# The order of ScalarE's work within a slot, and later slots for the norms, in an fp32 encoder trunk whose weights are split as they stream in

## The reference, cut to what matters

```python
def reference(...):                       # 512 prompt frames and 32 sample frames, D_MODEL = 1024, fp32
    for layer in range(2):
        g = norm_g[layer]
        xp, xs = rms_norm(hp, g[0]), rms_norm(hs, g[0])
        # layer 0: gated MLP and sliding-window attention with one output projection
        # layer 1: trailing mean pooling (windows 2, 4, 8, 16), then c_w, 4 groups of 256x256
        ...
        hp = hp + rms_norm(mp, g[1])
        hs = hs + rms_norm(ms, g[1])
        hp = hp + rms_norm(swiglu(rms_norm(hp, g[2]), ffn_w_in[layer], ffn_w_out[layer]), g[3])
        hs = hs + rms_norm(swiglu(rms_norm(hs, g[2]), ffn_w_in[layer], ffn_w_out[layer]), g[3])

def swiglu(h, w_in, w_out):               # w_in 1024 x 5632, w_out 2816 x 1024
    gu = h @ w_in
    return (jax.nn.silu(gu[..., :D_FF]) * gu[..., D_FF:]) @ w_out
```

## Time and profile before

| | |
|---|---|
| median of 3 runs | 1091.4 us (1090.87 to 1092.74) |
| the profiled execution | 1087.63 us, its span 1085.3 us |
| granted TensorE clock, mean | 0.994 |
| TensorE busy | 1045.7 us (96%) |
| VectorE busy | 623.3 us (57%) |
| ScalarE busy | 511.4 us (47%) |
| GpSimd busy | 50.8 us (5%) |
| HBM | 149 GB/s over the span |

### The profile page before, as it was taken

One profiled execution on the slowest core, in us unless ns is written; L12 is line 12 of the kernel. 1 busy time (PEld: TensorE's weight loads), 2 busy tenths in 40 slices (PEclk: granted clock), 3 DMA queues, 4 the chain that ended last, 5 costly groups with the idle time before them and its releaser, 6 DMA issues.

```text
span 1085.3 us, 19346 instructions
## 1 busy us (share of the span) xinstructions
PE 1045.7 (96%) x8087; PEld 1019.9 (94%) x8087; DVE 623.3 (57%) x920; ACT 511.4 (47%) x837; POOL 50.8 (5%) x52
## 2 busy tenths in 40 slices
PE   6999999899999999999989889999999999999997
PEld 4798889899999999999989889999999999999996
DVE  4377855777555545544456666667754545454543
ACT  5531355556444444445456445564544444444542
POOL 0070220000000000000000000200000000000000
PEclk9999999999999999999999999999999999999998
DMA  7413113456665555546654465454565555466552
GB/s 244 98 44 103 40 40 97 138 155 195 195 190 170 165 166 165 159 140 188 179 154 129 132 186 165 129 166 133 164 198 161 170 158 164 145 182 179 152 169 82
DMA packets 307636, 162.47 MB, mean 150 GB/s; under 512 B 14553, under 2 KB 304321, under 8 KB 307550
## 3 DMA queue, kind: packets, MB, share of 16 engines
q1 hardware_dynamic: 305678, 159.11, 50.3%
q10 hardware_dynamic: 1648, 1.78, 0.5%
q0 software_dynamic: 224, 0.35, 0.1%
HBM read 158.63 MB, written 2.58 MB: 149 GB/s over the span
## 4 chain that ended last, share of the span: by engine, by line
PE 78%; DVE 10%; issue 6%; ACT 3%; DMA 1%; POOL 1%; SPq 0%; ACTq 0%; DVEq 0%; POOLq 0%
PE ps L529 25%; PE ps L530 24%; PE ps L531 24%; DVE wlo L1435 3%; ACT whi L1049 2%; DVE tmp L1701 1%; DVE h L1705 1%; PE ps L569 1%; DMA x_tok<-in_x_sample_dram 1%; POOL rs L1946 1%; DVE acc L1687 1%; PE ps L786 1%; PE ps L946 0%; DVE tmp L1715 0%; PE ps L918 0%
## 5 line engine op out<-in xcount | busy, mean ns | idle before, releaser
L1435 DVE TENSOR_TENSOR wlo<-raw,whi 128x1024 fp32r<-128x1024 f32 (+2 forms) x332 | 369.0, 1112 | 309.1 <-ACT whi L1049 308.4
L529 PE MATMUL ps<-xhi,whi 128*128 128x288 f32 (+1 forms) x1600 | 466.5, 292 | 8.7 <-DVE wlo L1435 6.5
L530 PE MATMUL ps<-xlo,whi 128*128 128x288 f32 (+1 forms) x1600 | 462.9, 289 | 0.0
L531 PE MATMUL ps<-xhi,wlo 128*128 128x288 f32 (+1 forms) x1600 | 460.5, 288 | 0.0
L1049 ACT ACTIVATE whi<-raw 128x1024 fp32r<-128x1024 f32 (+2 forms) x332 | 315.1, 953 | 222.2 <-PE ps L531 191.2
L529 PEld LDWEIGHTS ps<-xhi,whi 128*128 128x128 f32 x1600 | 302.4, 189 | 12.2 <-DVE wlo L1435 7.4
L531 PEld LDWEIGHTS ps<-xhi,wlo 128*128 128x128 f32 x1600 | 302.8, 189 | 0.0
L530 PEld LDWEIGHTS ps<-xlo,whi 128*128 128x128 f32 x1600 | 302.6, 189 | 0.0
L529 PE MATMUL ps<-mhi_b,whi 128*128 128x288 f32 x352 | 105.7, 300 | 5.5 <-DVE wlo L1435 5.5
L531 PE MATMUL ps<-mhi_b,wlo 128*128 128x288 f32 x352 | 104.3, 296 | 0.0
L530 PE MATMUL ps<-mlo_b,whi 128*128 128x288 f32 x352 | 102.7, 292 | 0.0
(11 more groups left out here) (216 smaller groups left out, 944.8 us busy)
## 6 DMA issues: line engine op xcount, KB each, us to landing
raw<-in_ffn_w_in_dram SPq DMA_DIRECT2D x176, 512.0 KB, 3.9
raw<-in_ffn_w_out_dram SPq DMA_DIRECT2D x64, 384.0 KB, 3.5
raw<-in_ffn_w_out_dram SPq DMA_DIRECT2D x64, 320.0 KB, 3.1
raw<-in_ab_w_in_dram SPq DMA_DIRECT2D x10, 512.0 KB, 4.0
raw<-in_ab_w_out_dram SPq DMA_DIRECT2D x10, 256.0 KB, 2.8
raw<-in_ab_w_out_dram SPq DMA_DIRECT2D x20, 128.0 KB, 3.1
x_tok<-in_x_prompt_dram SPq DMA_DIRECT2D x4, 512.0 KB, 5.2
raw<-in_ab_w_in_dram SPq DMA_DIRECT2D x8, 256.0 KB, 3.5
```

The source lines that it names most:

```text
L529: pe.matmul(out, wh, xh, start=first, stop=False)
L530: pe.matmul(out, wh, xl, start=False, stop=False)
L531: return pe.matmul(out, wl, xh, start=False, stop=last)
L1435: dve.tensor_tensor(wlo[:, s, 0:n], raw[:, m % NRAW, 0:n], whi[:, s, 0:n].bitcast(F32), ALU.subtract)\
```

## The change

ScalarE's `square_pair` and `x_high` yield their slot plus 0.5 (`LATER`), and all passes call `run(slot + LATER)` behind `hi_part(m + 4)` (in odd slots of `ffn_in`, behind the high part of the product too). Squares and x high parts thus follow the slot's weight high part. VectorE's last `x_low` moves one slot on. In `STAGE`, the three stages of half 1 get two slots between `sum` and `spread` and between `pre` and `again` (in place of one), and what follows moves back by one to five slots; the `c` units of layer 1 come after units 22 and 24 in place of 19 and 21. In `after_mixer_ab` two of ScalarE's squares go behind a high part, and on VectorE the low parts of units + 9, + 10 and + 11 go behind the fold of the squares.

```diff
--- before.py
+++ after.py
@@ -81,17 +81,17 @@
 CARRY = 16
 
 
-C_AFTER = ((15, 16), (19, 21))
+C_AFTER = ((15, 16), (22, 24))
 STAGE = {
-    (0, 1): {"sum": 1, "spread": 2, "scale": (3, 5, 7, 9), "fold": 10, "pre": 12, "again": 13, "x": (14, 16, 18, 20)},
+    (0, 1): {"sum": 1, "spread": 3, "scale": (3, 5, 7, 9), "fold": 11, "pre": 13, "again": 15, "x": (15, 17, 19, 21)},
     (1, 0): {"sum": 0, "spread": 1, "scale": (1, 2, 3, 4), "fold": 6, "pre": 8, "rows": (7, 7, 8, 8),
              "keep": (9, 9, 10, 10), "bands": (11, 11, 12, 12, 13, 13, 14, 14)},
     (2, 0): {"sum": 20, "spread": 21, "scale": (21, 22, 23, 24), "fold": 26, "pre": 28, "again": 29,
              "x": (29, 30, 31, 32)},
-    (1, 1): {"sum": 1, "spread": 2, "scale": (2, 3, 5, 6), "fold": 8, "pre": 10, "rows": (8, 9, 9, 12, 12, 13),
-             "keep": (11, 11, 12, 12, 13, 13), "bands": (14, 14, 15, 15, 16, 16, 17, 17, 18)},
-    (2, 1): {"sum": 25, "spread": 26, "scale": (26, 27, 29, 30), "fold": 32, "pre": 34, "again": 35,
-             "x": (35, 36, 38, 39)},
+    (1, 1): {"sum": 2, "spread": 4, "scale": (4, 5, 7, 8), "fold": 10, "pre": 12, "rows": (10, 11, 11, 15, 15, 16),
+             "keep": (14, 14, 15, 15, 16, 16), "bands": (17, 17, 18, 18, 19, 19, 20, 20, 21)},
+    (2, 1): {"sum": 28, "spread": 30, "scale": (30, 31, 33, 34), "fold": 36, "pre": 38, "again": 40,
+             "x": (40, 41, 42, 43)},
     (3, 0): {"sum": 1, "spread": 2, "scale": (2, 4, 6, 8), "rows": (10, 10, 11, 11)},
 }
 
@@ -190,7 +190,7 @@
     return run
 
 
-LAST = 1 << 20
+LAST, LATER = 1 << 20, 0.5
 
 
 def shape_constants():
@@ -1243,11 +1243,11 @@
                 hi_part(U_OUT + 8)
                 square_pair(0, 0, 0)
                 evacuate_out(9)
+                hi_part(U_OUT + 9)
                 square_pair(0, 0, 1)
-                hi_part(U_OUT + 9)
-                square_pair(0, 0, 2)
                 evacuate_out(10)
                 hi_part(U_OUT + 10)
+                square_pair(0, 0, 2)
                 square_pair(0, 0, 3)
                 evacuate_out(11)
                 hi_part(U_OUT + 11)
@@ -1278,6 +1278,7 @@
                         pool_products(m, 1)
                         run(slot)
                         hi_part(m + 4)
+                        run(slot + LATER)
                         continue
                     f, j = divmod(UNITS[m][3], 2)
                     i = inner(layer, b, f)
@@ -1365,7 +1369,7 @@
                 if s == 3:
                     return
                 for p, slot in enumerate(at["scale"]):
-                    yield slot
+                    yield slot + LATER
                     square_pair(s, b, p)
                 if not power:
                     yield at["pre"]
@@ -1738,22 +1742,22 @@
                 add_z(0, 1, 2)
                 residual_pair(0, 0, 1)
                 lo_part(U_OUT + 8)
+                residual_pair(0, 0, 2)
                 add_z(0, 1, 3)
-                residual_pair(0, 0, 2)
-                lo_part(U_OUT + 9)
                 residual_pair(0, 0, 3)
-                add_z(0, 1, 4)
-                lo_part(U_OUT + 10)
                 add_square(0, 0, 3)
                 fold_squares(0, 0)
+                add_z(0, 1, 4)
+                lo_part(U_OUT + 9)
+                invert(0, 0, 1)
                 add_z(0, 1, 5)
-                lo_part(U_OUT + 11)
-                invert(0, 0, 1)
+                lo_part(U_OUT + 10)
                 dve.wait_ge(r_kept[0], KEPT[0, 1])
                 x_scale(0, 0, 0)
+                lo_part(U_OUT + 11)
+                x_low(0, 0, 0)
                 x_scale(0, 0, 1)
                 add_z(0, 1, 6)
-                x_low(0, 0, 0)
                 x_scale(0, 0, 2)
                 x_low(0, 0, 1)
                 lo_part(U_OUT + 12)
@@ -1867,6 +1871,7 @@
                     x_scale(s // 2, b, p)
                     if p:
                         x_low(s // 2, b, p - 1)
+                yield at["x"][-1] + 1
                 x_low(s // 2, b, 3)
 
             def pooling(b):
```

## The result

| | before | after |
|---|---|---|
| median of the runs | 1091.13 us (1089.12 to 1092.74, 4 runs) | 1063.47 us (1062.22 to 1065.39, 4 runs) |
| the profiled execution, its span | 1087.63, 1085.3 us | 1063.66, 1061.4 us |
| granted clock, mean of that execution | 0.994 | 0.996 |
| TensorE busy | 1045.7 us | 1037.8 us |

The ratio is 0.9749, interval 0.9727 to 0.9771: 27.7 us saved by the medians, 24.0 us between the two profiled executions. I had forecast 1071.6 us, a gain of 19.8, and a range that began at 1068. The sign and the mechanism held; the size was too small by 8 us of 28.

A forecast was written before the change was run, and what follows sets the result against it. TensorE, busy 1045.7 of 1085.3 us, was the bound, leaving only waits and lower clock to gain. Terms 3.3 + 6.2 + 1.5 + 2.1 + 7.5 - 0.3 - 0.5 = 19.8 us off 1091.4 gave 1071.6 us, range 1068 to 1078.

The forecast's parts named there:

- the ring: Norm slots passed between VectorE and ScalarE make weight low parts late; reordering in ffn_out(0, 1) removes 3.3 + 6.2 us.
- second drop: Lower clock at 696.92 us behind short matmuls: expected to stay, with 1.3 us as the gain if it falls away.
- the bands: Band low parts held up behind VectorE's product beside GpSimd's multiplication: third ring bank 0.3 us late, once.
- the cost of a wait: Each TensorE wait was taken to cost 0.17 us more than its row says.
- (a): VectorE becomes the bound in ffn_out(0, 1), low parts stay late: gives back 2.8 to 6 us, about 1076 us; chance 0.27.
- (b): ScalarE's order is of no account, only the GpSimd gaps count: 5.6 us gained, 1085.8 us; chance 0.05.
- (c): Squares last in the slot hold up silu or evacuation in ffn_in: 24 us lost, 1095 us; chance 0.04.
- thinnest cover: Second unit's low part at ffn_in(1, 0) ready about 1.2 us before TensorE arrives; failing, part of 2.8 us stays.
- `after_mixer_ab`: Reordering around the fold: no gain expected, a loss of 0.5 us; bounds a gain of 0.5 and a loss of 1.5.
- the step of the clock: Lower-clock time around ffn_in(1, 0): 1.5 us taken as gained, a further 1.3 us drop at 696.92 left in.
- first drop: Lower clock at the start of ffn_in(1, 0), behind the 2.8 us wait: 1.5 us taken as gone, bounds 0 and 1.5.
- the gaps: Two slots for GpSimd's power in (0, 1), (1, 1), (2, 1): 2.1 us with the fold's second wait, then 7.5 us.

The follow-up runs named there:

- order alone: Kernel before, with ScalarE's squares and x high parts behind the slot's weight high part, last x low part one slot later: 1064.95 us, ratio 0.9778.
- the squares alone: Kernel before, with only ScalarE's squares behind the slot's weight high part, x high parts still ahead of it: 1069.72 us, ratio 0.9823.
- old slots: Changed kernel with the stage slots and c units put back as before: 1066.01 us, ratio 0.9763 to the kernel before.
- old `after_mixer_ab`: Changed kernel with the order of after_mixer_ab put back as before: 1063.68 us, ratio 0.9767 to the kernel before.
- the gaps alone: Kernel before, with only the slots of the three stages of half 1 and the c units moved: 1087.11 us, ratio 0.9977.

## Why the prediction was right or wrong, point by point

**Right: the ring.** No low part is late in any of the three passes. `ffn_out(0, 1)`, up to the first matmul of the next pass, gained 10.45 us where I had 3.3 + 6.2 = 9.5; `ffn_in(1, 0)` 11.91 where I had 1.5 + 7.5 - 0.3 = 8.7; `ffn_in(0, 0)` 1.66 where I had 2.1 - 0.5 = 1.6. The surplus of 3.2 us in `ffn_in(1, 0)` is made up of terms below: the second drop of the clock, the bands, the cost of a wait and the pace of the matmuls. The prediction's figures for the scale slots there add up to some 14.7 us of VectorE's work, not 14, against TensorE's 14.1; it held all the same. The run with ScalarE's order alone keeps nearly all of the gain; rivals (a), (b) and (c) are out: VectorE does run without a gap, as (a) had it, but the three units ahead cover it; no silu or evacuation is waited for. The thinnest cover, 1.2 us at the second unit of `ffn_in(1, 0)`, was 1.1: low part ready at 618.65, pass begun at 619.74.

**Right: `after_mixer_ab`.** Sum 0.56 us earlier (0.5 placed), third unit 0.42 later (0.5 placed), two x waits of about 1.1 us between starts in place of one; I had 1.0 and 2.1 for them.

**Wrong: the step of the clock.** This is the term that put the time outside the range. I took 1.5 us for the first drop, left the second (1.3 us) in because the short matmuls ahead of it stay, and carried the sum over to the median as if the 3.8 us between profile and median had nothing to do with the change. The second drop went: in the profiled runs the two drops cost 3.1 us, counted by the starts of the same matmuls, not 1.5. In the four traces with the whole of ScalarE's order (after, order alone, old slots, old `after_mixer_ab`) the clock doesn't fall ahead of the tail. But it didn't fall behind the short matmuls in the unchanged kernel's second trace either, and it did in the one with the squares alone, so that the second drop is gone may in part be chance.

The rest is the way from the profile to the median. The profiled run of before lay 3.5 us below its median, after's at its own. The unchanged kernel gives a likely reason: its median run has 9.8 us of (1 - clock) x span against 6.8 in the profiled run of before, so typical runs hold more drops, which go with the idle stretches. That all of the 3.5 us is clock isn't shown: the tail is in these figures too (0.3 to 4.7 us of them in the traces), the four runs of before beside after have no clock on record, and the kernel's median was 1088.44, 1089.39 and 1091.97 us beside the other experiments. Beside those, the whole change less one of its parts gained 24.4 us (order alone), 26.0 (old slots) and 24.8 (old `after_mixer_ab`, which by its trace is the faster of the two), so one to three of the 27.7 may be a draw. Even without that step the sum was short: it gave 1067.8 for a run like the profiled one, and after's took 1063.66.

**Wrong: the cost of a wait.** 0.26 to 0.27 us over its row, not 0.17: the matmul behind the first one comes 0.1 us late too. Over the 13 waits of the sum that is 1.3 us.

**Wrong: whose wait it was.** I gave the gaps 2.1 us in (0, 1), with the fold's second wait, and part of the 7.5 us in (1, 1) and (2, 1), and 5.6 us of the price of rival (b) rests on that. The run with ScalarE's order alone removes the waits at 242, 246 and 762 us without a gap; the sum doesn't change, its parts do: the gaps have 2.2 to 2.8 us, the order the rest. The row named GpSimd because its power was the last link; VectorE, which makes its input and lagged, was the larger cause (3.2 us at 762, beside 1.0 us of a slower power). I had also not seen that the gaps alone would open a new wait of 3.4 us.

**Too careful: the bands beside GpSimd.** The 0.3 us did not come: no wait of TensorE there. VectorE from 674 us, beside GpSimd's products of 2.38 us (from 674.01) and 3.26 us (from 676.46):

```profile
674.85 2.62 DVE L1439 TENSOR_TENSOR wlo<-raw,whi 128x1024 fp32r<-128x1024 f32 x1 [2.56 <-ACT whi L1049]
677.39 0.41 DVE L1796 TENSOR_TENSOR tmp<-tmp,ps 128x256 f32<-128x256 f32 x1
677.72 0.87 DVE L1832 SCALAR_TENSOR_TENSOR xlo<-ps,gains,xhi 128x256 fp32r<-128x256 f32 x2
678.88 1.93 DVE L1439 TENSOR_TENSOR wlo<-raw,whi 128x1024 fp32r<-128x1024 f32 x1 [0.29 <-ACT whi L1049]
```

The weight's low parts, which read two operands from SBUF (where the weights and both parts of them lie), take 2.62 and 1.93 us in place of 1.23; the band's low parts, with one from PSUM (where the product of the band lies), take their usual 0.48 each. The Trainium skill, page "SBUF — State Buffer", section "Who interferes with whom", says just this, that an instruction of VectorE with at most one SBUF input (outside its two-port modes) does not contend with GpSimd. The trace agrees with it. I had this rule and took the row of an operation with two inputs all the same.

**The account.** Between the profiles 24.0 us: 19.8 of the sum, 1.3 for the second drop, 0.3 for the bands, 1.3 for the waits' cost; 1.3 us are left. About 0.7 of them are a pace that I can't explain: with no wait and the clock at 1.00, a matmul of 256 columns in `ffn_in` starts 117.8 or 118.9 ns after the one before it, for long stretches at a time, and after has more of the faster ones (mean of `ffn_in(0, 0)` 118.1 ns before and 117.8 after, of `ffn_in(1, 0)` 118.5 and 118.1). To the medians it is 3.7 us more, as told. What else than the clock makes the 1.7 us of spread in the kernel before stays open.

## What to carry to other kernels

In a slot that two in-order engines pass back and forth, put first what waits for nobody and feeds the other engine (here the weight's high part), and last what waits for the other engine; the waits of others that look like a slow third engine may vanish with it, so price them only after you have followed their input back. Where TensorE's stream is otherwise dense, a wait is dearer than its row: add what the next matmuls lose, and the clock, and read the clock from several runs, since one profiled execution shows only one draw of the drops. Parts of such a change do not add: test each both alone and taken back.

## What the runs showed of the hardware that I had not expected

- Ahead of the tail the granted clock falls to its lower level behind idle stretches of TensorE of 1.3 to 3.4 us, and in five of the twelve traces behind a stretch of short matmuls without a wait, but not at the same places in each run: at 632 and 697 us in one trace of the kernel before, at 195, 667 and 762 in another. The mean clock of runs of that kernel varied from 0.985 to 0.993.
- Filling seven waits with 46 matmuls that are thrown away made the kernel 0.74% faster (1082.49 beside 1091.97 us).
- GpSimd's power took 1.76 to 1.89 us where a low part of VectorE had started up to 0.16 us ahead of it (644 and 762 us of before), and 0.85 us where it started ahead of the low part (the trace with 46 fills).
- A lower clock in the tail costs little: all that follows `ffn_in(1, 0)` takes 293.5 us in before, with 3.4 us of (1 - clock) x span in it, and 293.4 us in the trace with 46 fills, with 0.5.
- The pace of TensorE in `ffn_in(0, 0)`, at clock 1.00 and without waits, is not the same in each run, 117.8 or 118.9 ns for a matmul of 256 columns: between 255 and 325 us it started 597 in before and 592 in the trace with 46 fills.
- A 128x128 fp32 matmul (the fill) is two passes, 0.112 us apart.
